# Recurrent stage of a hybrid decoder layer: chains started earlier, distances on VectorE, small levels in blocks of 32 by 32

## The reference, cut to what matters

```python
log_f = logaddexp(log(lb), log1p(-lb) + log_sigmoid(f))   # forget gate, per token and channel
k     = (1 - lb) * sigmoid(-f)
S_t   = diag(f_t) S_{t-1} + k_t v_t^T
o_t   = S_t^T q_t
```

## Time and profile before

| what | value |
|---|---|
| runs | 497.51, 500.89, 501.62 us; median 500.89 |
| profiled execution | 497.14 us, its span 495.3 us |
| mean granted TensorE clock | 0.997 |
| busy PE, PEld | 474.5, 386.5 us |
| busy DVE, ACT, POOL | 287.8, 209.5, 178.6 us |

### The profile page before, as it was taken

One profiled execution on the slowest core, in us unless ns is written; L12 is line 12 of the kernel. 1 busy time (PEld: TensorE's weight loads), 2 busy tenths in 40 slices (PEclk: granted clock), 3 DMA queues, 4 the chain that ended last, 5 costly groups with the idle time before them and its releaser, 6 DMA issues. The chain is left out here.

```text
span 495.3 us, 6784 instructions
## 1 busy us (share of the span) xinstructions
PE 474.5 (96%) x2566; PEld 386.5 (78%) x2566; DVE 287.8 (58%) x552; ACT 209.5 (42%) x350; POOL 178.6 (36%) x162
## 2 busy tenths in 40 slices
PE   3999999999999999999997999989999999999993
PEld 2778888889778889776886887778788888888882
DVE  3354589999991433334599775995170513363276
ACT  5364444323355254357463628542295322443000
POOL 0444433544356555464141103020016544795000
PEclk9999999999999999999999999999999999999998
DMA  8607222233022201220220220201204223456012
GB/s 288 233 2 267 79 81 86 85 97 119 41 86 87 87 20 66 86 71 16 86 75 12 86 85 1 85 23 64 85 24 146 85 89 105 140 176 258 1 65 105
DMA packets 15440, 45.69 MB, mean 92 GB/s; under 512 B 2056, under 2 KB 3504, under 8 KB 15408
## 3 DMA queue, kind: packets, MB, share of 16 engines
q1 hardware_dynamic: 14016, 44.06, 26.1%
q10 hardware_dynamic: 1392, 1.20, 0.7%
HBM read 43.14 MB, written 2.11 MB: 91 GB/s over the span
## 5 line engine op out<-in xcount | busy, mean ns | idle before, releaser
L1433 POOL TENSOR_TENSOR w_lo<-w_raw,w_hi 128x512 fp32r<-128x512 f32 x96 | 126.4, 1342 | 159.1 <-ACT w_hi L686 159.1
L396 PE MATMUL bank<-x_hi,w_hi 128*128 128x512 f32 x352 | 142.2, 404 | 0.1
L397 PE MATMUL bank<-x_lo,w_hi 128*128 128x512 f32 x352 | 137.9, 392 | 0.0
L398 PE MATMUL bank<-x_hi,w_lo 128*128 128x512 f32 x352 | 137.7, 391 | 0.0
L396 PEld LDWEIGHTS bank<-x_hi,w_hi 128*128 128x128 f32 x352 | 66.4, 189 | 19.7 <-issue 5.4
L398 PEld LDWEIGHTS bank<-x_hi,w_lo 128*128 128x128 f32 x352 | 66.4, 189 | 14.6
L397 PEld LDWEIGHTS bank<-x_lo,w_hi 128*128 128x128 f32 x352 | 66.5, 189 | 13.0 <-issue 0.5
L686 ACT ACTIVATE w_hi<-w_raw 128x1024 fp32r<-128x1024 f32 x64 | 66.0, 1052 | 8.1 <-PE bank L398 5.5
L769 ACT ACTIVATE prob<-prob,nmax 128x128 f32<-128x128 f32 (+3 forms) x32 | 17.8, 556 | 52.9 <-DVE nmax L1101 52.8
L1089 DVE COPY prob_t<-bank 128x128 f32<-128x128 f32 (+3 forms) x32 | 14.2, 486 | 40.1 <-PE bank L531 40.0
L396 PE MATMUL bank<-w_hi,x_hi 128*128 128x256 f32 x128 | 37.4, 292 | 0.0
(11 more groups left out here) (168 smaller groups left out, 769.0 us busy)
## 6 DMA issues: line engine op xcount, KB each, us to landing
w_raw<-in_w_units SPq DMA_DIRECT2D x68, 512.0 KB, 4.6
x_raw<-in_x_t SPq DMA_DIRECT2D x8, 256.0 KB, 7.0
x_res<-in_x_tok SPq DMA_DIRECT2D x4, 512.0 KB, 7.6
out<-y_sb SPq DMA_DIRECT2D x8, 256.0 KB, 2.0
t_turned<-t_row SPq DMA_DIRECT2D x1, 1024.0 KB, 9.7
ln_gb<-in_ln_g SPq DMA_DIRECT2D x1, 512.0 KB, 6.9
ln_gb<-in_ln_b SPq DMA_DIRECT2D x1, 512.0 KB, 8.9
kiwi_raw<-in_w_kiwi ACTq DMA_DIRECT2D x1, 288.0 KB, 3.8
```

What stands on the lines that cost most here:

```text
L396: nc.tensor.matmul(dst, a_hi, b_hi, start=first, stop=False)
L397: nc.tensor.matmul(dst, a_hi, b_lo, start=False, stop=False)
L398: return nc.tensor.matmul(dst, a_lo, b_hi, start=False, stop=last)
L1433: nc.gpsimd.tensor_tensor(split_target(u, kiwi_lo, x_lo, w_lo)[:, k, :], raw(u)[:, k, :], split_target(u, kiwi_hi, x_hi, w_hi)[:, k, :].bi ...
```

## The change

1. **Units.** `fa1` comes before `qa0`, so both forget projections are there by quarter 68.
2. **Early chains.** `forget` of pair p = 0 starts at quarter 64 and of p = 1 at 68 (three parts in three quarters; the p = 1 chain has buffers of its own, `dec_1` and `log_1`, and `k_a` holds all four heads). `Q_NEAR = (72, 78)` is a new stage number for `near_factors` (q-1), `near_products` (q) and `far_factors` (q+1). The wait for the end of attention is dropped for p = 0 and kept for p = 1.
3. **Distances on DVE.** All six level distances and the end distance of each pair run on DVE; POOL keeps none. The end distance is written into `k_l`. Unit 17 joins `LO_DVE`.
4. **Order.** `Q_TREE = (73, 82)`. `TREE_AT` spreads 11 steps over seven quarters; exponentials of a level stand one quarter ahead of its products, and the products one quarter ahead of its matmul. `recur` moves to `Q_TREE + 8` and what follows to `+ 9`.
5. **Blocks of 32 by 32.** The diagonal and levels h = 16 to 1 are multiplied in 32 matmuls with 32 columns each (to output partitions 0, 32, 64, 96), instead of 8 with 128 columns. One diagonal step serves both heads. They are gathered in `att_d` by one predicated copy per step, and `expand` on ACT copies `att_d` into `att` at the end, in four pieces. POOL clears `att` and `att_d` first (`clear_att`).
6. **Copies.** The levels h = 64 and 32 are moved to `att` by ACT instead of DVE.

The diff, cut to its core:

```diff
-         "ia0", "ia1", "fa0", "qa0", "fa1", "qa1", "ga0", "ga1", "ga2", "ga3",
+         "ia0", "ia1", "fa0", "fa1", "qa0", "qa1", "ga0", "ga1", "ga2", "ga3",
-TREE = [("diag", 0), ("diag", 1), ("lv", 0), ("lv", 1), ("128", 0), ("lv", 2),
-        ("256", 0), ("lv", 3), ("256", 1), ("lv", 4), ("lv", 5), ("lv", 6)]
+TREE = [("diag", 0), ("lv", 0), ("lv", 1), ("lv", 2), ("128", 0),
+        ("lv", 3), ("256", 0), ("lv", 4), ("256", 1), ("lv", 5), ("lv", 6)]
-Q_PREP = (68, 79)
-Q_TREE = (73, 84)
-Q_MERGE = Q_TREE[1] + 9
+Q_PREP = (64, 68)
+Q_NEAR = (72, 78)
+Q_TREE = (73, 82)
+TREE_AT = (0, 1, 1, 2, 3, 3, 4, 4, 5, 5, 6)
+Q_MERGE = Q_TREE[1] + 10
...
@@ PE, tree()
                 if kind == "diag":
                     pe.wait_ge(k_done, 2 * (p + 1))
-                    for t in range(TB):
-                        mm = nc.tensor.matmul(dst[:, queries(t)], k_a[:, m, queries(t)],
-                                              q_a[:, 2 * p + m, queries(t)], start=True, stop=True)
+                    wait_proj_out(pe, f"qa{p}", 0)
+                    wait_proj_out(pe, f"qa{p}", 1)
+                    for a in range(2):
+                        for t in range(TB):
+                            c = (a * TB + t) * 32
+                            for i in range(0, P, 32):
+                                block = slice(t * P + i, t * P + i + 32)
+                                mm = nc.tensor.matmul(dst[i:i + 32, c:c + 32], k_a[:, 2 * p + a, block],
+                                                      q_a[:, 2 * p + a, block], start=True, stop=True)
...
-                                parts = ((key, query, 0, 0),)
                                 if m == 1:
                                     parts = ((key[:, 0:32], query[:, 0:32], 0, 0),
                                              (key[:, 64:96], query[:, 32:64], 64, 32))
+                                else:
+                                    c = (a * TB + t) * 16
+                                    parts = [(key[:, 32 * i:32 * i + 32], query[:, 16 * i:16 * i + 16], 32 * i, 0)
+                                             for i in range(4)]
...
@@ ACT
                 nc.scalar.activation(q_r[:], cp, ACT.Exp).then_inc(rl_done, 1)
-                wait_dist(act, p, 0)
-                nc.scalar.activation(flat(k_l[:]), dec[:, 0, :], ACT.Exp).then_inc(rl_done, 1)
+                act.wait_ge(dist_end, p + 1)
+                nc.scalar.activation(k_l[:], k_l[:], ACT.Exp).then_inc(rl_done, 1)
...
-                for p in range(2):
-                    for lv in {0: (1,), 1: (2, 3), 2: (4,), 3: (5,), 4: (6,)}.get(q - Q_TREE[p], ()):
-                        level_factors(p, lv)
...
+                    if q == Q_NEAR[p] - 1:
                         near_factors(p)
+                for p in range(2):
+                    for lv in range(max(1, q - Q_TREE[p] + 2), min(6, q - Q_TREE[p] + 2) + 1):
+                        level_factors(p, lv)
...
+            def expand(p):
+                wait_tree_out(act, p)
...
+                for i in range(0, P, 32):
+                    block = strided(att[i:i + 32, 0, 0, i:i + 32], [[TB * SEQ, 2], [SEQ + P, TB], [1, 32]])
+                    nc.scalar.activation(block, att_d[i:i + 32], ACT.Copy).then_inc(att_done, 1)
...
@@ DVE
+            def end_distance(p):
+                if p:
+                    dve.wait_ge(far_done, 6)
+                    wait_lvl_multiplied(dve, 0, 0)
+                c = flat(cum[:, 2 * p:2 * p + 2, :]).rearrange("p (s t) -> p s t", t=SEG)
+                dve.wait_ge(cum_done, 2 * (p + 1))
+                nc.vector.tensor_tensor(flat(k_l[:]).rearrange("p (s t) -> p s t", t=SEG),
+                                        c[:, :, SEG - 1:SEG].broadcast_to([P, 2 * NSEG, SEG]), c,
+                                        ALU.subtract).then_inc(dist_end, 1)
...
+                    if q in (Q_PREP[p], Q_PREP[p] + 1, Q_PREP[p] + 2):
+                        forget(p, q - Q_PREP[p])
+                    if q == Q_NEAR[p] - 1:
+                        end_distance(p)
+                    if q == Q_NEAR[p]:
                         near_products(p)
+                    if q == Q_NEAR[p] + 1:
                         far_factors(p)
...
+                    if at == -1:
+                        distance(p, 1)
+                        distance(p, 2)
+                    if 1 <= at <= 5:
+                        level_products(p, at + 1)
+                    if 1 <= at <= 3:
+                        distance(p, at + 3)
                 for p, n in tree_at(q):
                     tree_place(p, n)
...
                         level_products(p, 1)
                         distance(p, 3)
+                    if at == 2:
                         far_products_128(p)
-                    if at == 1:
+                    if at == 3:
                         far_products_256(p)
...
-                for a in range(2):
-                    src = strided(bank[:, a * 256:a * 256 + 256], [[64, TB], [h, 64 // h], [1, h]])
-                    mask = strided(masks_sb[:, m - 2, :], [[0, TB], [h, 64 // h], [1, h]])
-                    ins = nc.vector.copy_predicated(att_blocks(a, h), mask, src)
-                ins.then_inc(log_out[idx % 2], 1)
+                src = strided(bank[:], [[16, 2 * TB], [h, 16 // h], [1, h]])
+                mask = strided(masks_sb[:, 16 * (m - 2):], [[0, 2 * TB], [h, 16 // h], [1, h]])
+                nc.vector.copy_predicated(later_halves(h), mask, src).then_inc(log_out[idx % 2], 1)
```

More of the change, by code:

```diff
@@ L837, in tree_copy @@
                 kind, m = TREE[n]
-                if kind not in ("128", "256"):
+                if kind == "diag" or (kind == "lv" and m >= 2):
                     return
@@ L841, in tree_copy @@
                 act.wait_ge(log_full, idx + 1)
+                bank = log_bank[idx % 2]
                 if p:
                     act.wait_ge(recur_done, 2)
-                bank = log_bank[idx % 2]
-                if kind == "128":
+                else:
+                    act.wait_ge(att_zero, 1)
+                if kind == "lv":
+                    h = LEVELS[m]
+                    for row, col in ((0, 0),) if m == 0 else ((0, 0), (64, 32)):
+                        keys = slice(row, row + h)
+                        src = bank[keys, :].rearrange("p (a t n) -> p a t n", a=2, t=TB)[:, :, :, col:col + h]
+                        base = att[keys, 0, 0, row + h:row + 2 * h]
+                        ins = nc.scalar.activation(strided(base, [[TB * SEQ, 2], [SEQ + P, TB], [1, h]]), src, ACT.Copy)
+                elif kind == "128":
                     for a in range(2):
@@ L1217, in tree_place @@
                 kind, m = TREE[n]
-                if kind not in ("diag", "lv"):
+                if kind in ("128", "256") or (kind == "lv" and m < 2):
                     return
@@ L1229, in tree_place @@
+                    nc.vector.copy_predicated(att_d[:].rearrange("p a t n -> p (a t) n"), mask,
+                                              strided(bank[:], [[32, 2 * TB], [1, 32]])).then_inc(log_out[idx % 2], 1)
                     return
+                before = ("lv", m - 1) if m > 2 else ("diag", 0)
+                wait_log_out(dve, TREE0 + NTREE * p + TREE.index(before))
                 h = LEVELS[m]
-                if m == 0:
-                    for d in range(2):
-                        wait_log_out(dve, TREE0 + NTREE * p + d)
-                else:
-                    link_level(p, m)
@@ L1491, in side @@
                     make_reset()
-                for p in range(2):
-                    if q == Q_PREP[p] + 2:
-                        end_distance(p)
-                    at = q - Q_TREE[p]
-                    if at == -1:
-                        distance(p, 2)
-                    if at == 1:
-                        distance(p, 4)
-                    if at == 3:
-                        distance(p, 6)
+                if q == Q_TREE[0] - 1:
+                    clear_att()
             for q in range(4 * NMAIN):
@@ L1523, in tree_level_masks @@
 def tree_level_masks():
[L1525 to L1526 removed]
+    key, n = np.arange(P)[:, None] % 32, np.arange(32)[None, :]
+    levels = [(key // (2 * h) == n[:, 0:16] // h) & (key % (2 * h) < h) for h in LEVELS[2:]]
+    return np.concatenate(levels + [key == n], 1).astype(np.int32)
 def kernel(**inputs):
```

174 lines of the change are left out of this document (74 added, 100 removed).

## The result

The changed kernel takes 485.49 us (median of 6 runs, 484.15 to 486.35) against 498.54 us for the kernel before (median of 6, 497.06 to 501.62). The ratio is 0.9745, 95% interval 0.9714 to 0.9775: 2.5% faster. The profiled execution took 486.19 us, its span 484.4 us.

What follows compares the result with a forecast made beforehand. PE, busy 96% of the span, was taken as the bound: 497.1 - 6.5 (PE work) - 5.4 + 5.7 (idle time) = 490.9 us profiled, scaled to a median of 494.6 and rounded to 494 us; range 486.5 to 503.

Steps and rivals of the forecast that it cites:

- PE work of the 32-column matmuls: Diagonal and levels h <= 16: 12 sets fall from 1.70 to 1.16 us each, 6.5 us less PE work.
- Rival B: Small-matmul sets: no gain in PE work, 1.70 us a set at 25 ns an instruction, about 501 us; chance 0.08.
- rival C: Small-matmul sets: neighbouring strips do not overlap, 33 ns an instruction, 2.2 us a set, 507 us; chance 0.05.
- Idle time: PE's waits in the tree stages: 5.4 us of old idle time removed, 5.7 us of new added.
- The stalls move rather than vanish: PE's idle time goes from both pairs into pair 0, its near stage behind pair 1's preparation: 5.7 against 5.4 us.
- No stall here costs clock: Both tree stages and the stretch behind them: granted clock 1.00 in all three, so waits lose no clock.
- Early stage: Quarters 64 to 72: PE runs through without waiting, reaching quarter 73 at 255.0 us.
- rival D: Early stage slips 2 to 3 us, pair 0's idle time doubles to 11 us: 500 us; chance 0.13 together with E.
- E: Distances on DVE as slow as POOL's 1.9 to 3.0 us, showing as rival D; chance 0.13 together with it.
- The thin covers: Before quarter 72: unit 18's weight pieces come 0.2 us before use at 256.4 us; otherwise PE waits a few tenths.
- Rival A: Quarters 73 to 76: DVE's and ACT's chains run 2 us earlier, stalls shrink, 5 us more go: 489.5 us; chance 0.14.
- DVE and POOL: POOL about 20 us less busy, DVE's total hardly moves, its near product at 1.2 us instead of 3.01.

Runs made afterwards that it cites:

- run 3: Changed kernel with each set's matmuls ordered one output strip after another (all of partitions 0 to 31 first): 497.06 us, ratio 0.9968.
- Run 4: Changed kernel with each set's matmuls taking two output strips in turn (0 and 64, then 32 and 96): 489.23 us, ratio 0.9805.
- run 5: Changed kernel with pair 0's end distance on DVE moved from quarter 71 to 69 and its near_factors on ACT from 71 to 70: 485.42 us.
- run 9: Changed kernel with the steps at distance 128 and 256 one quarter later, pair 0's near stage left at quarter 71: 485.25 us, ratio 0.9752.
- run 8: run 5 with the steps at distance 128 and 256 one quarter later for both pairs: 481.96 us, ratio 0.9685.
- run 1: Kernel before, old order and bank layout, with the 32-by-32 matmuls alone: 490.23 us, ratio 0.9827.
- run 7: Changed kernel with the distances of levels 2, 4 and 6 on POOL again: 486.72 us, ratio 0.9777.
- run 6: run 5 with the low parts of the weights of units 17 to 24 moved to POOL: 496.62 us, ratio 0.9957.
- run 2: Changed kernel's order, early chains and distances on DVE, with matmuls of 128 weight columns and 64 query columns: 494.92 us, ratio 0.9919.

## Why the prediction was wrong, step by step

- **PE work of the 32-column matmuls: the step that failed, by its size.** The prediction said "I take the same 16.5 ns" and 6.5 us. It was 8.4 ns and 12.4 us. The mechanism, narrow loads side by side, was right, and the prediction even gave the better end, "at best twice the rate, 0.63 us a set, 12.8 us in all", but did not forecast it. The row it rested on alternates between two strips; I read its pace as a property of the width. Runs 3 and 4 show that it was a property of the two strips: 1.83, 1.03 and 0.66 us for one, two and four. Run 4, which has the row's pattern, has a set of 1.03 us (1.16 forecast), and even so its ratio is 0.9805, with an interval that lies below the forecast's 0.988.
- **What this term explains of the number.** With 12.4 us in place of 6.5 the prediction's own sum gives 497.1 - 12.4 + 0.3 = 485.0 us, a ratio of 0.976, inside the measured interval. In time it gives 500.89 * 485.0 / 497.1 = 488.7 us, still inside the range. The last step below the range came from the base: six executions of before have a median of 498.54 us, the three known ahead had 500.89, and that takes off 2.3 us. Of the rest, idle time took 1.35 us more away and the half clock gave 1.7 back; about 1 us has no source that the runs show.
- **The floor of 25 ns.** Rival B is what the Trainium skill's floor would give, about 25 ns from start to start ("TensorE: Matmul & The Clock Gate", section "Wait — 56ns, not 53.3ns?"). The traces disagree where strips alternate, 8.4 ns, and come near it only when one strip is used, 1.83 / 64 = 28.6 ns (run 3). B fell, and rival C with it: neighbouring strips do overlap.
- **Idle time.** Forecast 5.7 us, measured 4.35 us, and each wait at its forecast place: the diagonal on ACT's `q_a` 0.8 us (1.35), level 1 on `k_c` 2.9 (2.5), the far matmuls on `far` 0.7 (1.75), pair 1 none (0.1). DVE's and ACT's chains ran as walked: the diagonal began at 259.29 us (259.1), level 1 at 266.99 (266.7), the far matmuls at 276.51 (276.0). What differed is when PE came. It was 0.6 us late from before quarter 68, which shortened the first wait, and ready for the far matmuls at 275.85 instead of 274.25 us, held up by the half clock, which shortened the last. So the idle time below the forecast is no merit of the new order: what PE did not wait before the far matmuls it had spent at half clock. "The stalls move rather than vanish" held; run 5 shows that `leave_bank` and most of level 1's wait came from the late `end_distance(0)`.
- **"No stall here costs clock": wrong for the new order.** It was read from the one profiled execution of before, with waits of at most 1.87 us, and the sum had no term for the clock. The new wait of 2.9 us was followed by 3 us at 0.50, for 1.7 us. The prediction walked to that wait and did not ask what it would do to the clock.
- **Early stage.** PE waited nowhere from quarter 60 to 72, and `end_distance(0)` was done at 257.5 us (257.4 walked): rival D fell, and E with it, the distances taking 1.2 us each on DVE. The thin covers held.
- **Rival A** (the stalls vanish, 489.5 us) was nearer to the measured time than the forecast, but by luck: idle time in pair 0 was 4.35 us, not the 0.7 that A asks.
- **DVE and POOL.** POOL is 21.8 us less busy (20 forecast), DVE 6.4 us less. With no POOL pass beside it the near product took 1.2 us, as forecast.
- **A slip in the chances.** Faster by over 1% was put at 0.66; A's 0.14 and five sixths of the forecast's 0.60 make 0.64.

## What to carry to other kernels

Splitting small matmuls into pieces of 32 weight columns paid here only where neighbours in the list go to different output strips, and the gain grew with the number of strips in turn; look at that pattern, not at the width alone, when a row of the trace is used as a price. When the bounding engine waits for a full second engine, moving one step earlier can merely move the wait: here a later step had to be put off too (runs 5, 9 and 8). And price a wait on TensorE with the clock that may be lost behind it: about 1.7 us here, behind waits of 1.87 to 2.9 us, and not behind every one of them.

## What the runs showed of the hardware

- 128 by 32 fp32 weight loads with their matmuls follow each other at 8.4 ns in four strips in turn (an fp32 matmul is recorded as two), and a set of 64 takes 0.66, 1.03 or 1.83 us by the order of strips alone.
- Idle times of PE of 2.2 us (run 5) and 2.9 us were followed by a stretch at 0.50 of the clock, and so was one of 1.87 us in run 1. One of 1.87 us in the kernel before, at the same step, and one of 2.6 us in run 7 were not. So the length of the wait alone doesn't decide it, and what does stays open.
- DVE passes beside POOL passes on other tiles can take longer, the smallest most: four passes of 2 elements took 2.77 us instead of 0.75 (run 6).
